# Squares of the head norms as a rounded and a remaining part, summed by two matmuls with ones

## The reference

```python
def rms_norm_2(x, g):
    xf = x.astype(jnp.float32)
    y = xf * lax.rsqrt(jnp.mean(xf * xf, axis=-1, keepdims=True) + EPS)
    return (y * g.astype(jnp.float32)).astype(x.dtype)
...
    (na_q, na_k, na_v, cq, ckv, k_rope, dq, dk, dv, z, gm) = jnp.split(h @ w_in_l, split_points, axis=-1)
    na_q = rms_norm_2(na_q.reshape(lead + (NA_HEADS, HEAD_DIM)), na_q_g)
    na_k = rms_norm_2(na_k.reshape(lead + (NA_HEADS, HEAD_DIM)), na_k_g)
...
    dq = rms_norm_2(dq.reshape(lead + (DIFF_HEADS, 2, DIFF_D)), diff_q_g)
    dk = rms_norm_2(dk.reshape(lead + (DIFF_HEADS, 2, DIFF_D)), diff_k_g)
```

## Time and profile before

| what | value |
|---|---|
| median of three runs | 2382.57 us |
| span of the profiled execution, first to last instruction | 2377.0 us |
| the profiled execution's own time | not shown apart from its span; the median lies 5.6 us above the span |
| TensorE matmuls busy | 2311.8 us, 97% |
| VectorE, ScalarE, GpSimd busy | 1570.0, 1216.2, 420.5 us |
| float32 sums of the head squares (L3223) | 64 records for 32 sums, 29.3 us |
| scaling of the tiles (L3250) | 32, 40.1 us |

### The profile page before, as it was taken

One profiled execution on the slowest core, in us unless ns is written; L12 is line 12 of the kernel. 1 busy time (PEld: TensorE's weight loads), 2 busy tenths in 40 slices (PEclk: granted clock), 3 DMA queues, 4 the chain that ended last, 5 costly groups with the idle time before them and its releaser, 6 DMA issues. The chain is left out here.

```text
span 2377.0 us, 35065 instructions
## 1 busy us (share of the span) xinstructions
PE 2311.8 (97%) x13734; PEld 1914.8 (81%) x13734; DVE 1570.0 (66%) x2386; ACT 1216.2 (51%) x2095; POOL 420.5 (18%) x272
## 2 busy tenths in 40 slices
PE   8998999999999999999999999999999999999999
PEld 5776788887889888799998767777767888778888
DVE  5967979778766666687676464643576465574685
ACT  3656545223328434567454355764366243576374
POOL 0000000000006444000002431004201126303301
PEclk9999999999999999999999999999999999999999
DMA  9734427666545332356664231223222333334344
GB/s 327 234 103 159 152 81 216 183 197 182 153 131 140 91 89 81 113 157 183 190 184 116 78 92 56 63 54 86 71 71 70 99 89 108 108 89 122 89 124 134
DMA packets 419340, 301.01 MB, mean 127 GB/s; under 512 B 13443, under 2 KB 389353, under 8 KB 419177
## 3 DMA queue, kind: packets, MB, share of 16 engines
q1 hardware_dynamic: 418064, 298.33, 43.5%
q10 hardware_dynamic: 1112, 0.44, 0.1%
HBM read 297.68 MB, written 1.05 MB: 126 GB/s over the span
## 5 line engine op out<-in xcount | busy, mean ns | idle before, releaser
L243 ACT ACTIVATE weights_hi<-wslots 128x1024 fp32r<-128x1024 f32 (+1 forms) x408 | 425.6, 1047 | 215.8 <-PE psum L306 180.1
L306 PE MATMUL psum<-input_hi,weights_hi 128*128 128x512 f32 (+1 forms) x1376 | 486.7, 354 | 1.5 <-PEq L1281 0.6
L306 PE MATMUL psum<-input_hi,weights_lo 128*128 128x512 f32 (+1 forms) x1376 | 474.9, 345 | 0.0
L306 PE MATMUL psum<-input_lo,weights_hi 128*128 128x512 f32 (+1 forms) x1376 | 474.6, 345 | 0.0
L253 DVE TENSOR_TENSOR weights_lo<-wslots,weights_hi 128x1024 fp32r<-128x1024 f32 x277 | 338.7, 1233 | 117.5 <-ACT weights_hi L243 116.7
L253 POOL TENSOR_TENSOR weights_lo<-wslots,weights_hi 128x1024 fp32r<-128x1024 f32 (+1 forms) x128 | 306.2, 2402 | 576.7 <-ACT weights_hi L243 576.1
L306 PEld LDWEIGHTS psum<-input_hi,weights_hi 128*128 128x128 f32 x1376 | 258.9, 188 | 42.9 <-issue 6.8
L306 PEld LDWEIGHTS psum<-input_lo,weights_hi 128*128 128x128 f32 x1376 | 259.1, 188 | 33.8 <-issue 2.6
L306 PEld LDWEIGHTS psum<-input_hi,weights_lo 128*128 128x128 f32 x1376 | 258.7, 188 | 33.0
L306 PE MATMUL psum<-ffn_hidden_hi,weights_hi 128*128 128x512 f32 (+1 forms) x512 | 172.3, 336 | 0.0
L306 PE MATMUL psum<-ffn_hidden_hi,weights_lo 128*128 128x512 f32 (+1 forms) x512 | 170.8, 334 | 0.0
(11 more groups left out here) (605 smaller groups left out, 4880.6 us busy)
## 6 DMA issues: line engine op xcount, KB each, us to landing
wslots<-w_in SPq DMA_DIRECT2D x130, 512.0 KB, 4.0
wslots<-ffn_w SPq DMA_DIRECT2D x128, 512.0 KB, 4.7
wslots<-ssd_w_in SPq DMA_DIRECT2D x49, 512.0 KB, 4.0
wslots<-ada_w SPq DMA_DIRECT2D x32, 512.0 KB, 4.7
h<-w_ada SPq DMA_DIRECT2D x28, 512.0 KB, 4.3
wslots<-gla_w_in SPq DMA_DIRECT2D x24, 512.0 KB, 4.9
input_raw<-ada_w SPq DMA_DIRECT2D x24, 512.0 KB, 4.1
ada_slab<-ada_w SPq DMA_DIRECT2D x24, 512.0 KB, 3.9
```

Of the source, the lines that this page charges most:

```text
L243: act.activation(self.high(self.whi_r, n), self.slot(n), ACT.Copy)\
L306: ins = pe.matmul(out_of(self.bank(g)), l, r, start=first and i == 0, stop=last and i == len(pairs) - 1, skip_group_check=not (first and l ...
```

## The change

The square of a tile is now split like a weight: ScalarE rounds it to a high part (`round_squares`), VectorE subtracts that and leaves a low part (`split_squares`), and TensorE sums both by two `float32r` matmuls with a rounded matrix of ones that accumulate into the same PSUM tile. `head_ones` is that matrix, written once over `half_ones`. `head_sq` is three buffers deep and takes the deviation too: it replaces `head_rstd`. So square n now waits until tile n-3 is normed, and no longer for a sum. `lag` becomes 3 in plain layer 0, and stays 2 in the differential stages and 3 in plain layer 1. The rope stage's small buffers move to other addresses.

```diff
-def sum_for_norm(b, pe, n, ones, sq, cols):
+def sum_for_norm(b, pe, n, ones, parts, cols):
-    rows = ones.shape[0]
-    pe.wait_ge(b.sem("squared"), b.nth("squared", n + 1))
+    pe.wait_ge(b.sem("squares_split"), b.nth("squares_split", n + 1))
     if n >= 2:
         pe.wait_ge(b.sem("deviation_ready"), b.nth("deviation_ready", n - 1))
     w = cols[1] - cols[0]
-    pe.matmul(b.psum[0:rows, 4 + n % 2, 0:w], ones, sq[0:rows, n % 2, 0:w], start=True, stop=True)\
-        .then_inc(b.tick("square_added"), 1)
+    o = b.psum[:, 4 + n % 2, 0:w]
+    hi, lo = (x[:, n % 2, 0:w].bitcast(F32R) for x in parts)
+    pe.matmul(o, ones[:].bitcast(F32R), hi, start=True, stop=False)
+    pe.matmul(o, ones[:].bitcast(F32R), lo, start=False, stop=True).then_inc(b.tick("square_added"), 1)
+def square_for_norm(b, pool, n, g, x, sq, cols):
     pool.wait_ge(*b.evacuated(g))
-    if n >= 2:
-        pool.wait_ge(b.sem("square_added"), b.nth("square_added", n - 1))
+    if n >= 3:
+        pool.wait_ge(b.sem("normed"), b.nth("normed", n - 2))
+    pool.tensor_tensor(sq[:, n % 3, 0:cols[1] - cols[0]], x, x, ALU.mult).then_inc(b.tick("squared"), 1)
+def round_squares(b, act, n, sq, hi, cols):
+    act.wait_ge(b.sem("squared"), b.nth("squared", n + 1))
+    if n >= 2:
+        act.wait_ge(b.sem("square_added"), b.nth("square_added", n - 1))
+    act.activation(hi[:, n % 2, 0:w].bitcast(F32R), sq[:, n % 3, 0:w], ACT.Copy).then_inc(b.tick("squares_rounded"), 1)
+def split_squares(b, dve, n, sq, hi, lo, cols):
+    dve.wait_ge(b.sem("squares_rounded"), b.nth("squares_rounded", n + 1))
+    dve.tensor_tensor(lo[:, n % 2, 0:w].bitcast(F32R), sq[:, n % 3, 0:w], hi[:, n % 2, 0:w], ALU.subtract)\
+        .then_inc(b.tick("squares_split"), 1)
 def deviation_for_norm(...):
     act.wait_ge(b.sem("square_added"), b.nth("square_added", n + 1))
-    if n >= 2:
-        act.wait_ge(b.sem("normed"), b.nth("normed", n - 1))
...
-        lag = 3 if joint else 2
+        lag = 2 if rope else 3
...
             def _(act):
                 b.round_weights(act, q0 + 1)
+                if not rope and l == 0:
+                    act.activation(ones[:].bitcast(F32R), b.half_ones[:], ACT.Copy)
                 for n in range(8):
                     b.round_weights(act, b.last_slot(qt + n) + AHEAD)
...
+                    if n:
+                        round_squares(b, act, n - 1, sq, sq_hi, cols[n - 1])
                     if n >= 3:
-                        deviation_for_norm(b, act, n - 3, rstd, P, cols[n - 3], 64)
+                        deviation_for_norm(b, act, n - 3, sq, cols[n - 3], 64)
+                round_squares(b, act, 7, sq, sq_hi, cols[7])
                 b.round_weights(act, v0 + VS - 1)
                 for n in range(5, 8):
-                    deviation_for_norm(b, act, n, rstd, P, cols[n], 64)
+                    deviation_for_norm(b, act, n, sq, cols[n], 64)
...
-                for n in range(8):
-                    scale_for_norm(b, dve, n, tile(n), rstd, P, cols[n], column(b, gains[n // 4], l))
+                for n in range(8 + 2):
+                    if n < 8:
+                        split_squares(b, dve, n, sq, sq_hi, sq_lo, cols[n])
+                    if n >= 2:
+                        scale_for_norm(b, dve, n - 2, tile(n - 2), sq, cols[n - 2], column(b, gains[(n - 2) // 4], l))
```

More of the change, by code:

```diff
@@ L439, in build @@
         b.ident = b.sb(ctx, "ident", [P, P])
+        b.turn_at = nc.sbuf_base
         b.snake = b.sb(ctx, "snake", [P, P])
         b.ones = b.sb(ctx, "ones", [P, P])
+        b.head_ones_at = nc.sbuf_base
         b.half_ones = b.sb(ctx, "half_ones", [P, P])
@@ L1374, in layer_input_norm @@
     with st:
-        b.sb(st, "heads_room", [P, 4, T])
+        b.sb(st, "heads_room", [P, 7, T])
         stat = b.sb(st, "in_stat", [P, 9, 2])
@@ L3222, in sum_for_norm @@
     w = cols[1] - cols[0]
-    pe.matmul(b.psum[0:rows, 4 + n % 2, 0:w], ones, sq[0:rows, n % 2, 0:w], start=True, stop=True)\
-        .then_inc(b.tick("square_added"), 1)
-def square_for_norm(b, pool, n, g, x, sq, rows, cols):
-    pool.wait_ge(*b.evacuated(g))
+    o = b.psum[:, 4 + n % 2, 0:w]
+    hi, lo = (x[:, n % 2, 0:w].bitcast(F32R) for x in parts)
+    pe.matmul(o, ones[:].bitcast(F32R), hi, start=True, stop=False)
+    pe.matmul(o, ones[:].bitcast(F32R), lo, start=False, stop=True).then_inc(b.tick("square_added"), 1)
@@ L3231, in square_for_norm @@
     w = cols[1] - cols[0]
-    pool.tensor_tensor(sq[0:rows, n % 2, 0:w], x, x, ALU.mult).then_inc(b.tick("squared"), 1)
-def deviation_for_norm(b, act, n, rstd, rows, cols, width):
+    act.activation(hi[:, n % 2, 0:w].bitcast(F32R), sq[:, n % 3, 0:w], ACT.Copy).then_inc(b.tick("squares_rounded"), 1)
+def split_squares(b, dve, n, sq, hi, lo, cols):
+    dve.wait_ge(b.sem("squares_rounded"), b.nth("squares_rounded", n + 1))
+    w = cols[1] - cols[0]
+    dve.tensor_tensor(lo[:, n % 2, 0:w].bitcast(F32R), sq[:, n % 3, 0:w], hi[:, n % 2, 0:w], ALU.subtract)\
+        .then_inc(b.tick("squares_split"), 1)
@@ L3236, in deviation_for_norm @@
+def deviation_for_norm(b, act, n, rstd, cols, width):
     act.wait_ge(b.sem("square_added"), b.nth("square_added", n + 1))
-    if n >= 2:
-        act.wait_ge(b.sem("normed"), b.nth("normed", n - 1))
     w = cols[1] - cols[0]
[L3240 to L3246, removed]
+    act.activation(rstd[:, n % 3, 0:w], b.psum[:, 4 + n % 2, 0:w], ACT.Sqrt, bias=b.eps[:, 1:2], scale=1.0 / width)\
+        .then_inc(b.tick("deviation_ready"), 1)
@@ L3247, in scale_for_norm @@
+def scale_for_norm(b, dve, n, x, rstd, cols, gain):
+    r = rstd[:, n % 3, 0:cols[1] - cols[0]]
     dve.wait_ge(b.sem("deviation_ready"), b.nth("deviation_ready", n + 1))
@@ L3278, in project_heads @@
     with st:
-        sq = b.sb(st, "head_sq", [P, 2, T])
-        rstd = b.sb(st, "head_rstd", [P, 2, T])
+        sq, sq_hi, sq_lo = (b.sb(st, f"head_{x}", [P, n, T]) for x, n in (("sq", 3), ("sq_hi", 2), ("sq_lo", 2)))
+        nc = b.nc
+        if not rope and l == 0:
+            b.head_ones = nc.alloc_sbuf_tensor_at("head_ones", [P, P], F32, offset=b.head_ones_at)
+        ones = b.head_ones
         if rope:
             tab = b.sb(st, "rope_tab", [P, 2, NLAT])
-            turn = b.sb(st, "rope_turn", [P, P])
-            tmp = b.sb(st, "rope_tmp", [P, 2, NLAT])
-            prod = b.sb(st, "lam_prod", [64, 2])
+            turn = nc.alloc_sbuf_tensor_at(f"rope_turn_{l}", [P, P], F32, offset=b.turn_at)
+            tmp = sq[:, 0:2, 0:NLAT]
+            prod = nc.alloc_sbuf_tensor_at(f"lam_prod_{l}", [64, 2], F32, offset=SBUF_TOP - 64)
         cols = [seg] * 4 + [ALL] * 4
         joint = kind == "na" and l == DEPTH - 1
-        lag = 3 if joint else 2
+        lag = 2 if rope else 3
         def tile(n):
@@ L3313, in _ @@
                     b.split_weights(pool, "pool", q0 + n + AHEAD)
-                    square_for_norm(b, pool, n, qt + n, tile(n), sq, P, cols[n])
+                    square_for_norm(b, pool, n, qt + n, tile(n), sq, cols[n])
                 b.split_weights(pool, "pool", z0 + 3 + AHEAD)
@@ L3332, in _ @@
                     if n >= lag:
-                        sum_for_norm(b, pe, n - lag, b.half_ones[:], sq, cols[n - lag])
+                        sum_for_norm(b, pe, n - lag, ones, (sq_hi, sq_lo), cols[n - lag])
                 for s in range(VS):
@@ L3336, in _ @@
                     if s < lag:
-                        sum_for_norm(b, pe, 8 - lag + s, b.half_ones[:], sq, cols[8 - lag + s])
+                        sum_for_norm(b, pe, 8 - lag + s, ones, (sq_hi, sq_lo), cols[8 - lag + s])
                 for j in range(4):
```

## The result

The changed kernel takes 2395.42 us, the median of four runs (2394.57 to 2398.07), beside 2382.73 for the kernel before: a ratio of 1.006 (95% interval 1.0049 to 1.0072), 12.7 us slower. A second series gave 2395.45 against 2381.06, ratio 1.0055 (1.0042 to 1.0069). The forecast was 2391.1, 8.5 slower: the sign was right, and so were the places inside the four stages; the size was a third too small.

The account below looks back on a forecast made before the run. TensorE, busy 97% of a 2377.0 us span, was taken to bound the kernel. Stage terms 1.3 + 3.9 + 4.3 + 1.7 - 2.7 = +8.5 us on the 2382.57 median gave 2391.1 us, range 2378 to 2397.

Parts of the forecast that it names:

- I take that once, **+1.7: Plain layer 1, behind TensorE's 7 us stop: work lost to a lower granted clock, 1.7 us, counted once.
- TensorE's own gain: All four head stages: two new matmuls cost less than one float32 sum, 14.0 us saved with nothing waiting.
- The ring: Layer 0: each square waits on the square before it through rounding, split and norming, 8.1 us a tile (bounds 6.6 and 8.1).
- Waits in layer 0: TensorE waits 6.1 us in plain layer 0 against 4.8 saved, and 7.6 in the differential stage against 3.7.
- third rival: Layer 0 stages end at the lower clock level and layer 1 loses twice as much: 13.6 us slower, 2396.2 us; chance 0.12.
- The stop in plain layer 1: Ahead of sum 0 of plain layer 1, TensorE waits 7.1 us for tile 0's queued rounding and split.
- The clock behind it: Plain layer 1, after the 7 us stop: TensorE partly at 1.2 GHz, 1.7 us of work lost.
- The ends that I had named: Limits for the clock loss behind plain layer 1's stop: nothing, and 3.4 us for twice as long.
- Differential layer 1: Short ring, `lag` 2 and no input norm beside it: all splits in time, 2.7 us gained.
- more clock lost: Rival: layer 0 stages end at the lower clock, layer 1 loses twice as much; 13.6 us slower, 2396.2 us; chance 0.12.
- no wait for GpSimd: Rival: VectorE's split does not wait for GpSimd, layer 0's ring is 6.6 us; 3.9 us faster, 2378.7 us; chance 0.15.
- no stops: Rival: sums stay off every wait in all four stages, all 14.0 us gained, 2368.6 us; chance 0.10.

Follow-up runs that it names:

- all_three: Changed kernel with two float32 sums in plain layer 1, GpSimd's weights split behind the head split, and deviation in its own buffers: 2364.53 us, ratio 0.9936.
- own_deviation: Changed kernel with the deviation in two buffers of its own again and the low part written over the square: 2377.91 us, ratio to before 0.9988.
- two_sums_only: Kernel before with its float32 sum replaced by two rounded-type matmuls that both read the square, no rounding or split: 2370.30 us, ratio 0.9959.
- joint_kept_busy: Changed kernel with eight float32 matmuls of ones run on TensorE ahead of sum 0 of plain layer 1: 2390.28 us, ratio to before 1.005.
- changed kernel again: The changed kernel run once more, nothing altered, for a second profile: 2395.45 us against 2381.06 for before, ratio 1.0055.
- joint_two_whole: Changed kernel with the sums of tiles 0 and 1 in plain layer 1 float32 again, waiting for the square alone: 2381.77 us, ratio to before 1.0001.

## Why the prediction was right in kind and short in size

The step that failed is the term "I take that once, **+1.7**" for the clock behind the stop of plain layer 1. It measured 2.3 to 2.8 us. It is the largest miss that has a cause, but it is not all of the missing 4.2 us. By stages the misses are 0.4, 0.7, 1.2 and 0.2, together 2.5. The remaining 1.7 (3.7 in the second series) stand outside the four stages, where the forecast carried the change of the stages over to the medians and added nothing. Term by term:

- *TensorE's own gain*, 14.0 with nothing waiting: right. all_three, which gives 0.5 of it up for two float32 sums, gains 13.4; own_deviation gives 4.9 and 3.6 in layer 0, the differential stage of layer 1 gave 2.5 to 2.8 in every version with both sums, two_sums_only 12.1 in all without the `lag`.
- *The ring*, 8.1 us a tile: right (8.15). Both parts of its working hold when taken away singly: without GpSimd's hold 6.63, without the shared buffer none. The Trainium skill ("SBUF — State Buffer", section "SBUF: two separate sides") has VectorE wait for the whole instruction of GpSimd; the trace agrees, since the split ends 0.55 us after GpSimd's, that is nearly its whole 0.69.
- *Waits in layer 0*, 6.1 and 7.6: the stages lost 6.6 and 8.3 against own_deviation, 0.5 and 0.7 more than forecast. The first profile of the changed kernel shows 4.1 us of stops in the plain stage and the second 5.4, with the stage equally long: where the ring sets the pace, a slower clock falls into the next stop, as said under the third rival. For the plain stage the total is better than its working: the forecast put 3.2 us ahead of sums 5 and 6, and the traces have 2.27 ahead of a v product that it didn't name and 0 and 0.79 ahead of these sums. That the total came out near is in part luck.
- *The stop in plain layer 1*, 7.1: right (7.01, and 7.01 again), and for the reason given.
- *The clock behind it*, "I take that once, +1.7": this is the term that was mis-sized. It was read from a single stop of 2.48 us; after 7 us the lower level held for 5 to 5.6 us of TensorE's work, 2.5 and 2.8 us lost, and joint_kept_busy gave 2.3 to 2.6 back. The trace of before had the warning: behind its stop of 2.26 us at 2024.29 the clock cost 3.4. The ends that I had named, nothing and 3.4, hold the measured price. What is left of the stage is +4.6 with the clock kept up (forecast 4.3).
- *Differential layer 1*, -2.7: right (-2.5).

The four stages explain 11.0 and 10.7 us of a difference of 12.7 and 14.4 by the medians. What lies between, 2 to 4 us, is in no place that I can show: across all versions medians and stages differ by up to 4 us either way (changed kernel again +3.7, joint_two_whole -2.6), and only for joint_two_whole and all_three does a profile show where. So the cause stays open, and I don't call it a cost of the change. The rival "more clock lost" was half right in layer 1 (2.3 to 2.8, between the 1.7 taken and its 3.4) and not needed in layer 0; "no wait for GpSimd" and "no stops" each became true in a kernel that was made so, not in this one.

## What to carry to other kernels

A matmul that becomes cheaper by being split hands its price to the engines beside it: look first at what the new operation waits for, and at which buffer now has a second tenant. One shared buffer turned 6.3 us of VectorE's work a tile (2.22 + 3.34 + 0.76) into a ring of 8.15. If VectorE works on two SBUF operands beside GpSimd, put GpSimd's long operation behind it, next to one with a single operand. Don't price the clock behind a stop from one row: look at all stops of the trace. And where the gain is half a per cent, compare stages, not spans.

## What the runs showed of the hardware that was not expected

- After a stop of 7.0 us TensorE worked on at 1.2 GHz for 5 to 5.6 us in the changed kernel's two profiles; eight idle matmuls in the stop kept 2.4 GHz throughout.
- GpSimd's 2.4 us split and VectorE's reciprocal of 3.35 us run side by side with neither longer. GpSimd is held as well as holding: its square took 1.38 in place of 0.64 us beside a split of VectorE (1973.49 in the changed kernel).
- The same wait of 2.26 us for the softmax, in the first attention behind plain layer 1, was followed by 3.4 us of work lost to the clock in six profiles (both of before among them), 1.7 in four, and none in two.
- Identical code ahead of the first head stage took from 2.8 us less to 7.3 us more than in the first profile of before, and the granted clock goes with it. Half of the time that TensorE worked there at 1.2 GHz is 9.5 us in that profile, 15.9 in the one at +7.3, 14.8 at +4.4 and 7.8 at -2.8. The second profile of before fits least (8.0 at +1.2).
